# Opening slabs of four projections in pairs of chunks with 512 moving columns, and two low parts moved to GpSimd

## The chip, the core and the metric

The kernel runs on one core of a Trainium2 chip. The metric is device time in microseconds (us): 1195.06 us is the median of three runs (1194.7 to 1195.49).

## The reference

Everything is float32 on 256 tokens of 1024 features. The first block has two layers and a final norm, the second block one layer and a final norm; the second takes the first's output.

```python
# first block
x = x + even_mixer(rms_norm(x, norm_mix[0]), ...)    # neighbourhood attention (8 heads) and latent attention (8 heads)
x = x + sq_relu_mlp(rms_norm(x, norm_mlp[0]), ...)   # square(relu(xn @ w1)) @ w2, w1: 1024 x 4096
x = x + odd_mixer(rms_norm(x, norm_mix[1]), ...)     # dilated attention, 3 groups x 16 heads; w_in: 1024 x 9216
x = x + sq_relu_mlp(rms_norm(x, norm_mlp[1]), ...)
x = rms_norm(x, norm_final)
# second block
proj = rms_norm(x, mix_norm_gain_2) @ w_in_2         # to xa, ga (each 512), q, k, v (each 512), qx (512), gates (3072)
# linear recurrence on xa, causal attention on q k v, attention of qx to a memory of 256 tokens,
# three gated branches, w_out_2; then a gated feed-forward with a causal convolution, and a norm
```

The memory's keys and values, `rms_norm(mem_2) @ w_mem_kv_2`, depend on nothing else and are computed beside the first layer's attention.

## The kernel before

**Products in two parts.** For its precision the kernel splits each operand of a large product into a high part (rounded to the type that TensorE reads) and a low part (the rest), and adds three products: high by high, low by high, and high by low. A weight matrix is cut into 192 slabs of 1 MB, mostly 8 chunks of 128 rows by 256 columns, held in a ring of five raw buffers. SyncE loads slab n once slab n - 5 is released. ScalarE makes the high part (`high`, L1230; three buffers, so slab n needs slab n - 3 released). VectorE, or GpSimd for those slabs that `pooled` names, subtracts to get the low part (`low`, L1720 and L2486, on GpSimd in four pieces). `ahead(n)` means the split of slab n + 2; where it stands in an engine's program sets the order. Slabs 10, 12, 15, 17 (EVO) are the first layer's output projection, slabs 11, 13, 14, 16 (MEM) the memory's projection.

**The activations.** The high and the low part of the eight chunks of x lie side by side in XHL, 512 columns a chunk. ScalarE writes a high part (L1262), VectorE the low one from it (L1758, in the dilated order L1763).

**Three forms of a product with 256 columns of weights.**
- `features_by_chunks` (L695) takes two slabs together as the chunks of x come. Each slab has one bank of PSUM, its two halves of 128 features side by side. For each pair of chunks it issues high by high, low by high, high by low: for two slabs 96 matmuls of 256 moving columns, two banks.
- `beside` (L610, L615) gives each half slab a bank. The high weights are multiplied with XHL, 512 columns, so the bank's left half has high by high and its right half high by low; then the low weights add 256 columns to the left half. ScalarE copies the right half out (`copies`, L1286) and VectorE adds the left half to the copy (`added`, L1861). A bank is taken when VectorE has added it.
- `features_low_last` (L637) is the old form for slabs 2 to 5 of the third block, one bank a slab.

**Banks.** All eight PSUM banks go round in the order of use:

```python
i = turn_no[0] % 8
turn_no[0] += 1
if used[i] is not None:
    once.wait_ge(*at(("taken", *used[i])))
```

Uses other than slabs are `rows_back` (L909: transposes of the MLP's result, one bank each, added to x by VectorE at L1875), `last_rows_back` (two of these, issued between the first and second pair of chunks of the next product), the sums for a norm (L716, L720; one bank each), attention's scores, transposes and values.

**Order of work.** Each engine has its own program, run strictly in the order written; semaphores tie them. TensorE's order is: attention of the first layer with slabs between its steps, the MLP (`mlp`), the dilated part (`odd_slab`, i counts its 36 slabs), the second MLP, the third block's 12 slabs (IN2 = 122), its attention with the gates, the output projection, the feed-forward. `features_by_chunks` opens both MLPs, the dilated part and the third block. In the MLPs the pair is followed by ScalarE's Relu (L1364) and VectorE's square (L1893) for slabs 0 and 1, and by `copies`, `added` and one fused square (L1896) for the others. In the dilated part ScalarE copies a slab (L1526) for the exchange of rotary halves, and VectorE scales the slab out of PSUM (L2132; L2137 where `added` came first). In the third block VectorE runs `factors()` (L1747, L1753, L2224 to L2233: a mean, two reciprocals, four small operations, and one weight split within) and then `scaled` (L2215), which reads the slab and multiplies it with the factor. The feed-forward keeps `features_by_chunks`.

**Some waits of SyncE.** The exchange of rotary halves is four 64 KB transfers after ("copied", slab), queued before the slab load of its turn; the copy is of ScalarE before, and GpSimd multiplies what arrives (L2562).

The functions that the diff touches:

Of the kernel before, what the change touches and what calls it, by code (L numbers as in the profile page):

```python
# [336 lines left out]
def build(nc, A, out):  # L337
    with ExitStack() as ctx:
# [124 lines left out]
        def pooled(n):  # L463

            name = plan[n][0]
            if name == "od_o":
                return n >= ODO + 2
            if name == "branch":
                return sum(p[0] == "branch" for p in plan[:n]) > 1
            return name in ("out2", "fg")  # L470
# [101 lines left out]
        def tensor(pe):  # L572
# [128 lines left out]

            def tokens(n, x, late=False):
# [228 lines left out]
            def mlp(layer, norm, slot):  # L931
                features_by_chunks([W1[layer], W1[layer] + 1], x_ready(f"mlp{layer}"))
                row_sums(norm, slot)
                for j in range(2, 16):
                    beside(W1[layer] + j, x_ready(f"mlp{layer}"))
                down(layer, W2[layer])
# [123 lines left out]
            def odd_slab(i):  # L1060
                n, (kind, hb, g, k) = SLAB_ODD + i, DILATED[i]
                if i == 0:
                    features_by_chunks([n, n + 1], x, lambda: last_rows_back(0))
# [52 lines left out]
            for n in range(12):  # L1116
                if n == 0:
                    features_by_chunks([IN2, IN2 + 1], x, lambda: last_rows_back(1))
# [98 lines left out]
        def scalar(act):  # L1217
# [139 lines left out]
            def mlp(layer, norm, slot, follow):  # L1357
                for j in range(16):
# [3 lines left out]
                    if j < 2:  # L1362
                        b = take(("slab", W1[layer] + j))
                        act.activation(TA[j % 2][:, :], b[:, :], ACT.Relu).then_inc(  # L1364
                            *tell(s_act_out, ("taken", "slab", W1[layer] + j), ("relu", layer, j)))
                    else:
                        copies(W1[layer] + j, TB[j % 2], ("hlo", layer, j - 2))
                        ahead(W1[layer] + j + 1)
# [141 lines left out]
            def odd_slab(i, begun=False):  # L1510
# [13 lines left out]
                if i < 2:  # L1524
                    b = take(("slab", n))
                    act.activation(TA[k][:, :], b[:, :], ACT.Copy, scale=1.0).then_inc(*tell(s_act_out, ("copied", n)))  # L1526
                else:
                    copies(n, TA[k], ("rotated", swaps[0] - 2))
# [45 lines left out]
            for n in range(12):  # L1574
                if n != 1:
                    ahead(IN2 + n)
                if n == 0:
# [3 lines left out]
                    act.activation(RS[:, 0, 0:S + 2], RS[:, 0, 0:S + 2], ACT.Sqrt).then_inc(*tell(s_root, "both sqrt"))  # L1581
                if n == 7:
# [129 lines left out]
        def vector(dve):  # L1712
# [164 lines left out]
            def mlp(layer, norm, slot, follow, beside):  # L1877
                r = RS[:, slot, S:S + 2]
                for j in range(16):
# [11 lines left out]
                    if j < 2:  # L1891
                        once.wait_ge(*at(("relu", layer, j)))
                        dve.tensor_tensor(z, a, a, ALU.mult).then_inc(*tell(s_dve, ("h", layer, j)))  # L1893
                    else:
                        added(W1[layer] + j, a, z)
                        dve.scalar_tensor_tensor(out=z, in0=a, scalar=0.0, in1=a, op0=ALU.max, op1=ALU.mult).then_inc(  # L1896
                            *tell(s_dve, ("h", layer, j)))
# [210 lines left out]
            def odd_slab(i):  # L2108
# [5 lines left out]
                if 1 < i < EARLY:  # L2114
                    rotate(1)
                if i != 1:
                    ahead(n)
                rotate(1)
                if i == 0:
# [10 lines left out]
                if i < 2:  # L2130
                    b = take(("slab", n), [("copied", n)])
                    dve.tensor_tensor(to, pair(b[:, :]), twice(RP[:, 0:S]), ALU.mult).then_inc(  # L2132
                        *tell(s_dve_out, ("taken", "slab", n), ("scaled", n)))
                else:
                    v = TA[rotated[0] % 2]
                    added(n, v, v, ("copied", n))
                    dve.tensor_tensor(to, pair(v[:, :]), twice(RP[:, 0:S]), ALU.mult).then_inc(*tell(s_dve, ("scaled", n)))  # L2137
# [71 lines left out]
            def scaled(n, dst, by=1.0):  # L2209
                if n < IN2 + 8:  # L2210
# [264 lines left out]
        def gpsimd(pool):  # L2475
# [68 lines left out]
            for n in (EVO[2], MEM[3], EVO[3]):  # L2544
# [190 lines left out]
```

## Time and profile before

| | |
|---|---|
| median of 3 runs | 1195.06 us |
| the profiled execution | 1195.08 us |
| its span | 1193.3 us |
| TensorE, matmuls | 1184.5 us busy, 99% |
| TensorE, weight loads (beside the matmuls) | 1034.6 us, 87% |
| VectorE | 830.7 us, 70% |
| ScalarE | 658.5 us, 55% |
| GpSimd | 222.3 us, 19% |
| DMA queues | 54.6% of 16 engines, 214 MB |

A profile row gives the time of an instruction or of a run of like ones. The end of a matmul is modelled and includes its way through the array, so that successive matmuls overlap: their rate is read from start to start, or from the chain, which counts only the time to the next one. In all rows times are us from the span's start. In a timeline a row is: start, duration from first start to last end, engine, line, operation, output <- inputs, shapes, count, and in brackets an idle time of the engine before it and what ended it. Line numbers are those of the kernel before.

### The profile page before, as it was taken

The numbers are of one execution on the slowest core, as the hardware profiler recorded it, in microseconds if no ns is written. First come the engines' busy times: TensorE is split into PE (matmuls) and PEld (weight loads), VectorE is DVE, ScalarE is ACT, GpSimd is POOL, SyncE is SP. The second block draws the span as 40 slices with busy tenths as digits, with TensorE's granted clock in tenths as the row PEclk, the third lists the DMA queues.
The fourth block names the chain that finished last, engine by engine and source line by source line (L and its number), as shares of the span: only waits on it lengthen the run. The fifth ranks groups of instructions, "written<-read, shape, count | busy, mean of one in ns | idle before, by whom it ended". The sixth has DMA issues, their size and how long they took to land.

```text
span 1193.3 us, 18415 instructions
## 1 busy us (share of the span) xinstructions
PE 1184.5 (99%) x7409; PEld 1034.6 (87%) x7409; DVE 830.7 (70%) x1184; ACT 658.5 (55%) x899; POOL 222.3 (19%) x169
## 2 busy tenths in 40 slices
PE   9999999999999999999999999999999999999998
PEld 9989898888898888888988888897878899888886
DVE  7878777754576688765788844597966566676863
ACT  5584465533455655557565535456685555555452
POOL 2530010000011021200300000010010885544100
PEclk9999999999999999999999999999999999999999
DMA  9723456656558566664366565555544455565551
GB/s 265 244 83 130 141 177 186 203 178 205 182 165 273 187 211 193 202 204 140 110 190 198 178 204 184 185 183 176 178 144 166 149 194 177 182 195 188 176 195 53
DMA packets 158995, 214.04 MB, mean 179 GB/s; under 512 B 5259, under 2 KB 111054, under 8 KB 158910
## 3 DMA queue, kind: packets, MB, share of 16 engines
q1 hardware_dynamic: 158110, 211.41, 54.6%
q8 instruction: 59, 0.97, 0.3%
q10 hardware_dynamic: 608, 0.99, 0.3%
q0 software_dynamic: 192, 0.46, 0.2%
q14 instruction: 26, 0.21, 0.1%
HBM read 205.50 MB, written 1.05 MB: 173 GB/s over the span
## 4 chain that ended last, share of the span: by engine, by line
PE 93%; DVE 4%; ACT 2%; issue 1%; DMA 1%; SPq 0%; DVEq 0%; ACTq 0%
PE ps L595 44%; PE ps L610 22%; PE ps L615 11%; PE ps L695 4%; PE ps L792 2%; PE ps L843 2%; PE ps L637 2%; PE ps L800 1%; DVE wlo L1720 1%; PE ps L811 1%; PE ps L661 1%; ACT whi L1230 1%; DMA raw<-in_ev_w_in_dram 1%; DVE TA L2400 0%; PE ps L716 0%
## 5 line engine op out<-in xcount | busy, mean ns | idle before, releaser
L1720 DVE TENSOR_TENSOR wlo<-raw,whi 128x2048 fp32r<-128x2048 f32 (+1 forms) x167 | 384.5, 2304 | 148.9 <-ACT whi L1230 148.3
L1230 ACT ACTIVATE whi<-raw 128x2048 fp32r<-128x2048 f32 x188 | 357.9, 1907 | 154.4 <-PE ps L595 132.3
L610 PE MATMUL ps<-XHL,whi 128*128 128x512 f32 x1248 | 311.1, 393 | 0.0
L610 PEld LDWEIGHTS ps<-XHL,whi 128*128 128x128 f32 x1248 | 225.3, 189 | 42.1 <-DVE BIG L2132 0.5
L615 PEld LDWEIGHTS ps<-XHL,wlo 128*128 128x128 f32 x1248 | 167.8, 190 | 11.8 <-DVE wlo L1720 1.1
L615 PE MATMUL ps<-XHL,wlo 128*128 128x256 f32 x1248 | 171.5, 282 | 0.3 <-DVE wlo L1720 0.2
L2486 POOL TENSOR_TENSOR wlo<-raw,whi 128x512 fp32r<-128x512 f32 x88 | 119.1, 1388 | 157.3 <-ACT whi L1230 157.1
L595 PE MATMUL ps<-whi,HL 128*128 128x512 f32 (+1 forms) x416 | 144.8, 373 | 0.0
L595 PE MATMUL ps<-whi,HH 128*128 128x512 f32 x384 | 143.3, 390 | 0.0
L595 PE MATMUL ps<-whi,XHL 128*128 128x512 f32 (+1 forms) x480 | 139.7, 378 | 0.0
L595 PE MATMUL ps<-wlo,HH 128*128 128x512 f32 x368 | 139.4, 389 | 0.0
L595 PEld LDWEIGHTS ps<-whi,XHL 128*128 128x128 f32 x480 | 85.9, 188 | 15.9 <-issue 0.7
L2562 POOL TENSOR_TENSOR TB<-TB,BIG 128x512 f32<-128x512 f32 x24 | 38.6, 1607 | 324.3 <-DVE BIG L2126 189.1
L595 PEld LDWEIGHTS ps<-whi,HL 128*128 128x128 f32 x416 | 76.1, 188 | 13.6
L595 PE MATMUL ps<-wlo,XHL 128*128 128x512 f32 (+1 forms) x240 | 87.8, 375 | 0.0
L595 PEld LDWEIGHTS ps<-whi,HH 128*128 128x128 f32 x384 | 71.9, 188 | 14.7
L595 PEld LDWEIGHTS ps<-wlo,HH 128*128 128x128 f32 x368 | 69.0, 188 | 14.6 <-DVE wlo L1720 0.4
L1286 ACT ACTIVATE TB<-ps 128x256 f32<-128x256 f32 x82 | 29.3, 378 | 58.0 <-PE ps L615 56.2
L1286 ACT ACTIVATE TA<-ps 128x256 f32<-128x256 f32 x66 | 23.4, 380 | 57.5 <-PE ps L615 45.1
L595 PEld LDWEIGHTS ps<-wlo,XHL 128*128 128x128 f32 x240 | 44.2, 188 | 8.3
L1861 DVE TENSOR_TENSOR TA<-ps,TB 128x256 f32<-128x256 f32 x56 | 23.2, 421 | 25.0 <-ACT TB L1286 24.7
L1296 ACT ACTIVATE SN<-SN,stat 128x384 f32<-128x384 f32 (+2 forms) x64 | 34.4, 544 | 10.1 <-DVE stat L1789 10.1
(281 smaller groups left out, 1652.6 us busy)
## 6 DMA issues: line engine op xcount, KB each, us to landing
raw<-in_mlp_w_dram SPq DMA_DIRECT2D x64, 1024.0 KB, 5.3
raw<-in_od_w_in_dram SPq DMA_DIRECT2D x36, 1024.0 KB, 5.4
raw<-in_w_in_dram SPq DMA_DIRECT2D x24, 1024.0 KB, 5.1
raw<-in_w_ffn_gate_dram SPq DMA_DIRECT2D x12, 1024.0 KB, 5.1
raw<-in_w_ffn_up_dram SPq DMA_DIRECT2D x12, 1024.0 KB, 5.1
raw<-in_w_ffn_down_dram SPq DMA_DIRECT2D x12, 1024.0 KB, 5.0
TB<-TA SPq DMA_DIRECT2D x96, 64.0 KB, 2.4
raw<-in_w_branch_dram SPq DMA_DIRECT2D x6, 1024.0 KB, 4.9
```

The costliest lines, as they stand in the source:

```text
L595: m = pe.matmul(to, l[c][a], r[c][b], start=first and k == 0, stop=last and k == 3 * n - 1)
L610: pe.matmul(b[m][:, :], w[m][c][0], XHL[:, c, :], start=c == 0, stop=False)
L615: i = pe.matmul(b[m][:, 0:S], w[m][c][1], x[c][0], start=False, stop=c == 7)
L637: i = pe.matmul(b[:, m * S:m * S + S], w[m][c][a], x[c][z], start=m == c == a == z == 0, stop=m == a == 1 and c == len(x) - 1)
L695: i = pe.matmul(b[n][:, m * S:m * S + S], h[a], x[c][z], start=m == c == a == z == 0, stop=m == 1 and c == 7 and z == 1)
L792: m = pe.matmul(banks[u][rows, lo:hi], l, r, start=start, stop=stop)
L1230: act.activation(whi_of(n), raw_of(n), ACT.Copy, scale=1.0).then_inc(*tell(s_whi, ("whi", n)))
L1286: act.activation(to[:, m * S:m * S + S], b[:, S:2 * S], ACT.Copy, scale=1.0).then_inc(*tell(s_act_out, ("copy", n, m)))
L1296: m = act.activation(to[:, lo:hi], src[:, lo:hi], ACT.Exp, bias=st[:, k:k + 1], scale=-1.0 if biased else 1.0, accum_out=st[:, 2 + k:3 + k])
L1720: dve.tensor_tensor(wlo_of(n), raw_of(n), f32(whi_of(n)), ALU.subtract).then_inc(*tell(s_wlo, ("wlo", n)))
L2486: m = pool.tensor_tensor(lo[:, v], r[:, v], f32(hi[:, v]), ALU.subtract)
L2562: pool.tensor_tensor(z, z, twice(RP[:, S:512]), ALU.mult).then_inc(*tell(s_pool, ("sine", k)))
```

## The change

Four calls of `features_by_chunks` become calls of a new function, `pair_beside`, with four banks for two slabs. Its first pair of chunks goes (chunk 0 high weights), (0 low), (1 low), (1 high), the others low, low, high, high:

```diff
+            def pair_beside(ns, x, between=None):
+                b = {(n, m): bank(("beside", n, m)) for n in ns for m in range(2)}
+                w = {(n, m): w_ready(n, 8, m * P, P) for n in ns for m in range(2)}
+                for p in range(4):
+                    if p == 1 and between is not None:
+                        between()
+                    for c, a in ((0, 0), (0, 1), (1, 1), (1, 0)) if p == 0 else ((2 * p, 1), (2 * p + 1, 1), (2 * p, 0), (2 * p + 1, 0)):
+                        for n, m in b:
+                            for event in (w[n, m][c][2 + a], x[c][2], *((x[c][3],) if a == 0 else ())):
+                                once.wait_ge(*at(event))
+                            if a:
+                                pe.matmul(b[n, m][:, 0:S], w[n, m][c][1], x[c][0], start=False, stop=False)
+                            else:
+                                i = pe.matmul(b[n, m][:, :], w[n, m][c][0], XHL[:, c, :], start=c == 0, stop=c == 7)
...
-                features_by_chunks([W1[layer], W1[layer] + 1], x_ready(f"mlp{layer}"))
+                pair_beside([W1[layer], W1[layer] + 1], x_ready(f"mlp{layer}"))
...
-                    features_by_chunks([n, n + 1], x, lambda: last_rows_back(0))
+                    pair_beside([n, n + 1], x, lambda: last_rows_back(0))
...
-                    features_by_chunks([IN2, IN2 + 1], x, lambda: last_rows_back(1))
+                    pair_beside([IN2, IN2 + 1], x, lambda: last_rows_back(1))
```

What follows these products takes the form of the other slabs. MLP, ScalarE and then VectorE:

```diff
-                    if j < 2:
-                        b = take(("slab", W1[layer] + j))
-                        act.activation(TA[j % 2][:, :], b[:, :], ACT.Relu)...
-                    else:
-                        copies(W1[layer] + j, TB[j % 2], ("hlo", layer, j - 2))
+                    copies(W1[layer] + j, TB[j % 2], *([("hlo", layer, j - 2)] if j > 1 else []))
...
-                    if j < 2:
-                        once.wait_ge(*at(("relu", layer, j)))
-                        dve.tensor_tensor(z, a, a, ALU.mult).then_inc(*tell(s_dve, ("h", layer, j)))
-                    else:
+                    added(W1[layer] + j, a, z)
+                    dve.scalar_tensor_tensor(out=z, in0=a, scalar=0.0, in1=a, op0=ALU.max, op1=ALU.mult)...
```

Dilated part, VectorE (for the first two slabs the addition stands ahead of the next weight split; ScalarE makes two copies of the right halves in place of one of the whole):

```diff
+                if i < 2:
+                    v = TA[rotated[0] % 2]
+                    added(n, v, v, ("copied", n))
                 if i != 1:
                     ahead(n)
                 rotate(1)
```

Third block, ScalarE (behind the square root of the combined scale) and VectorE (in `scaled`, behind `factors()`):

```diff
+                if n < 2:
+                    copies(IN2 + n, PT[:, n, :])
...
             def scaled(n, dst, by=1.0):
-                if n < IN2 + 8:
+                if IN2 + 2 <= n < IN2 + 8:
                     b = take(("slab", n), ["both"])
                 else:
                     b = PT[:, (n - IN2) % 3, :]
                     added(n, b, b)
```

The low parts of slabs 14 (memory, third) and 15 (output projection, third) go from VectorE to GpSimd:

```diff
             name = plan[n][0]
+            if n in (EVO[1] + 2, MEM[1] + 2):
+                return True
...
-            for n in (EVO[2], MEM[3], EVO[3]):
+            for n in (EVO[1], MEM[1]):
                 ahead(n)
```

## Rows read from the trace of the kernel before

**Rows 1.** The page: TensorE's busy time, and the chain that ended last, by engine

```profile
PE   1184.5 (99%) x7409; PEld 1034.6 (87%) x7409; DVE 830.7 (70%) x1184; ACT 658.5 (55%) x899; POOL 222.3 (19%) x169
PE 93%; DVE 4%; ACT 2%; issue 1%; DMA 1%; SPq 0%; DVEq 0%; ACTq 0%
```

**Rows 2.** TensorE's waits: for whom, us in total, times, longest

```profile
PE ps L843 <- DVE PT L1812: 1.1, 2, 0.8
```

**Rows 3.** Timeline of TensorE around the second of these waits

```profile
127.76 0.28 PE L595 MATMUL ps<-wlo,HL 128*128 128x256 f32 x1
128.88 1.08 PE L843 MATMUL ps<-PT,BIG 128*64 128x256 f32 x8 [0.85 <-DVE PT L1812]
```

**Rows 4.** Timeline of VectorE: two weight splits, slab 14's first

```profile
111.84 2.29 DVE L1720 TENSOR_TENSOR wlo<-raw,whi 128x2048 fp32r<-128x2048 f32 x1
...
158.46 2.43 DVE L1720 TENSOR_TENSOR wlo<-raw,whi 128x2048 fp32r<-128x2048 f32 x1 [1.84 <-ACT whi L1230]
```

**Rows 5.** Timeline of ScalarE: the high part of slab 15

```profile
118.84 1.94 ACT L1230 ACTIVATE whi<-raw 128x2048 fp32r<-128x2048 f32 x1
```

**Rows 6.** Groups by line and shape: busy us, mean ns, idle before

```profile
L2486 POOL TENSOR_TENSOR wlo<-raw,whi 128x512 fp32r<-128x512 f32 x88 | 119.1, 1388 | 157.3 <-ACT whi L1230 157.1
L1861 DVE TENSOR_TENSOR TA<-ps,TB 128x256 f32<-128x256 f32 x56 | 23.2, 421 | 25.0 <-ACT TB L1286 24.7
```

**Rows 7.** The chain in order of time: start, us, what

```profile
39.49 3.65 PE ps L610 x16
43.14 1.91 PE ps L615 x16
...
149.44 11.72 PE ps L695 x96
...
589.19 11.59 PE ps L695 x96
```

**Rows 8.** Timeline of VectorE: low parts of x, both MLPs

```profile
149.37 0.88 DVE L1758 SCALAR_TENSOR_TENSOR XHL<-XT,V,XHL 128x256 fp32r<-128x256 f32 x2 [0.65 <-ACT XHL L1262]
...
589.35 2.70 DVE L1758 SCALAR_TENSOR_TENSOR XHL<-XT,V,XHL 128x256 fp32r<-128x256 f32 x4
```

**Rows 9.** Timeline of TensorE: the first product of both MLPs

```profile
149.41 1.19 PE L695 MATMUL ps<-XHL,whi 128*128 128x256 f32 x8
...
589.02 1.12 PE L695 MATMUL ps<-XHL,whi 128*128 128x256 f32 x8
```

**Rows 10.** Timeline of TensorE: high products of the fourth and the following slab, dilated

```profile
346.45 4.16 PE L610 MATMUL ps<-XHL,whi 128*128 128x512 f32 x16
...
352.36 3.82 PE L610 MATMUL ps<-XHL,whi 128*128 128x512 f32 x16
```

**Rows 11.** Timeline of VectorE: the scaling of the first two dilated slabs

```profile
347.75 1.29 DVE L2132 TENSOR_TENSOR BIG<-ps,BIG 128x512 f32<-128x512 f32 x2
```

**Rows 12.** Timeline of TensorE: slabs 2 and 4 of the third block begin

```profile
781.28 4.07 PE L637 MATMUL ps<-XHL,whi 128*128 128x256 f32 x32
...
792.87 4.00 PE L637 MATMUL ps<-XHL,whi 128*128 128x256 f32 x32
```

**Rows 13.** Timeline of VectorE: first and last step of factors(), and the first scaling

```profile
781.75 0.42 DVE L1747 TENSOR_SCALAR RS<-ps 128x258 f32<-128x258 f32 x1
...
789.59 0.43 DVE L2233 TENSOR_TENSOR RS<-RS 128x258 f32<-128x258 f32 x1
790.06 1.29 DVE L2215 SCALAR_TENSOR_TENSOR BIG<-ps,RS 128x512 f32<-128x512 f32 x2
```

**Rows 14.** Busy time by stretch at the kernel's end; PEclk is the granted clock

```profile
1187.00:1188.00 1.00, 0.41 (x2) 0.00 (x0) 1.00 (x2) 0.69 (x1) 0.00 (x0) 1.00 0.00 0
...
1191.00:1192.00 1.00, 0.00 (x0) 0.00 (x0) 0.00 (x0) 0.00 (x0) 0.00 (x0) 0.50 1.01 379
```

**Rows 15.** Timeline of TensorE: the same product at the start and later

```profile
1.04 4.64 PE L943 MATMUL ps<-ones 128*128 128x128 f32 x20 [1.04 <-DVE ones L1923]
...
7.07 1.60 PE L943 MATMUL ps<-ones 128*128 128x128 f32 x12
```

More of the change, by code:

```diff
@@ L700, in features_by_chunks @@
                     released[n] = [("product", "slab", n)]
+            def pair_beside(ns, x, between=None):
[12 more added lines that the diff above has]
+                                i = pe.matmul(b[n, m][:, :], w[n, m][c][0], XHL[:, c, :], start=c == 0, stop=c == 7)
+                            if c == 7 and a == 0:
+                                i.then_inc(*tell(s_product, ("product", "beside", n, m)))
+                for n in ns:
+                    released[n] = [("product", "beside", n, 1)]
             def tokens(n, x, late=False):
@@ L1361, in mlp @@
                         ahead(W1[layer] + 1)
-                    if j < 2:
-                        b = take(("slab", W1[layer] + j))
-                        act.activation(TA[j % 2][:, :], b[:, :], ACT.Relu).then_inc(
-                            *tell(s_act_out, ("taken", "slab", W1[layer] + j), ("relu", layer, j)))
-                    else:
-                        copies(W1[layer] + j, TB[j % 2], ("hlo", layer, j - 2))
+                    copies(W1[layer] + j, TB[j % 2], *([("hlo", layer, j - 2)] if j > 1 else []))
+                    if j > 1:
                         ahead(W1[layer] + j + 1)
@@ L1523, in odd_slab @@
                 k = swaps[0] % 2
-                if i < 2:
-                    b = take(("slab", n))
-                    act.activation(TA[k][:, :], b[:, :], ACT.Copy, scale=1.0).then_inc(*tell(s_act_out, ("copied", n)))
-                else:
-                    copies(n, TA[k], ("rotated", swaps[0] - 2))
+                copies(n, TA[k], *([("rotated", swaps[0] - 2)] if i > 1 else []))
                 swaps[0] += 1
@@ L1890, in mlp @@
                     a, z = TA[j % 2][:, :], TB[j % 2][:, :]
-                    if j < 2:
-                        once.wait_ge(*at(("relu", layer, j)))
-                        dve.tensor_tensor(z, a, a, ALU.mult).then_inc(*tell(s_dve, ("h", layer, j)))
[L1894 to L1897, printed above, removed]
+                    added(W1[layer] + j, a, z)
+                    dve.scalar_tensor_tensor(out=z, in0=a, scalar=0.0, in1=a, op0=ALU.max, op1=ALU.mult).then_inc(
+                        *tell(s_dve, ("h", layer, j)))
                     if j == 0:
@@ L2118, in odd_slab @@
                 rotate(1)
+                if i > 1:
+                    v = TA[rotated[0] % 2]
+                    added(n, v, v, ("copied", n))
                 if i == 0:
@@ L2129, in odd_slab @@
                 to = pair(QKV[hb % 3][3 * g + w])
[L2130 to L2137, printed above, removed]
+                v = TA[rotated[0] % 2]
+                dve.tensor_tensor(to, pair(v[:, :]), twice(RP[:, 0:S]), ALU.mult).then_inc(*tell(s_dve, ("scaled", n)))
                 if i >= EARLY:
```

## The prediction

> **What bounds the kernel now.** I read the page's busy shares first, then the chain that ended last, then the waits of TensorE, and last the timelines of the five places that the change touches. TensorE is busy for 99% of the span, and 93% of the chain runs through it [rows 1]. So the kernel is a queue of matmuls with hardly a hole: TensorE's longest entry in the waits is 1.1 us in two pieces, both for the copy of attention probabilities on VectorE [rows 2]. An edit can therefore gain only by shortening the stream of matmuls or by closing one of the few holes, and it loses one for one whatever it makes TensorE wait. VectorE (70%) and ScalarE (55%) have slack on the mean, which matters only where TensorE needs something of theirs.
>
> The sum is made against the profiled execution: 1195.08 us, of which 1193.3 are its span. The median of the three timed runs is 1195.06, so nothing has to be shifted between the two. Differences under 0.2% (2.4 us) can't be told from no change.
>
> **Part 1, two low parts on GpSimd.** Slabs 14 and 15 are split on GpSimd, in four pieces of 1.39 us each [rows 6], instead of one VectorE subtraction of 2.3 us each. VectorE did slab 14's at 111.84 [rows 4] and slab 15's in the same way between the two holes, each in front of the reductions, outputs and probability copies for which TensorE then waited. Taking away 2.2 us ahead of the first wait and 4.4 ahead of the second is more than both waits hold. The recorded waits are 1.1 us; from the issue times the second hole alone is 128.88 - 127.76 - 0.12 = 1.0 [rows 2, 3]. I take 1.25 us of gain, bounds 0.8 and 1.5. Is the low part late? The high part of slab 15 is ready at 118.84 + 1.94 = 120.8, GpSimd ends at 120.8 + 4 x 1.39 = 126.4, and slab 15 is multiplied only after the values and transposes issued from 128.88 [rows 3, 5, 6]. Slab 14 has more room. GpSimd has nothing else to do between the rotary keys and the squares of the first MLP. So no wait replaces the ones removed.
>
> The Trainium skill ("GPSIMD Engine Reference", Key points) speaks against such a move: GpSimd shares its SBUF interfaces with VectorE and contends with instructions that have two SBUF inputs. The trace shows a little of it: the VectorE subtraction that began at 158.46, with GpSimd at work, took 2.43 us instead of 2.29 [rows 4]. By that ratio (6%) some 8 us of VectorE work beside GpSimd would lengthen by 0.5 us, which the 4.4 us it was relieved of cover; the sum stays.
>
> **Part 2, the pair products.** Before, two slabs took 96 matmuls of 256 columns; after, 32 of 512 and 32 of 256, the same columns in fewer instructions. In the chain 16 matmuls of 512 take 3.65 us and 16 of 256 take 1.91, so a pair costs 2 x 3.65 + 2 x 1.91 = 11.12 us; the 96 took 11.72 and 11.59 in the two MLPs [rows 7]. The gain is 0.47 to 0.60 us a pair, and there are four pairs.
>
> The Trainium skill ("TensorE: Matmul & The Clock Gate", Back-to-back issue gap) gives N/2.4 + 2.5 ns for the isolated spacing. By it 32 instructions fewer are 0.08 us. Here 1.91/16 - 256/2.4 is 12.7 ns, so the measurement decides.
>
> Where does the gain go? The new order opens with a product of the high weights with both parts of chunk 0, so it needs chunk 0's low part; the old one needed the high part alone.
> - First MLP: the low parts of chunks 0 and 1 are two operations of 0.88 us together from 149.37, so chunk 0's ends at about 149.85, and the first matmul goes at about 149.98 instead of 149.41. That is 0.57 later, against 0.47 to 0.6 shorter [rows 7 to 9]. With the later chunks (the pair needs two more of them every 11.12 / 4 = 2.8 us, and the old run of 11.72 us with the same steps had hardly a hole) nothing more is late. I take +0.1.
> - Second MLP: there the four low parts begin at 589.35, after a weight split, and the old code began at 589.02. First matmul at about 589.96: +0.94 - 0.47 = +0.5 [rows 7 to 9].
> - In both MLPs VectorE gets two additions of 0.42 us [rows 6] for each of the two slabs and keeps its square. That is 1.6 us more ahead of the split of slab 5 of the MLP. By my walk along the queue it keeps 1 us of room in the first MLP and nearly none in the second, where the decay steps are interleaved. I count 0, bounds 0 and 0.4.
> - Dilated part: chunk 0's two parts are long there. The shorter pair ends 0.47 earlier, but the fourth slab's second half already waited for a bank: 16 matmuls took 4.16 us instead of 3.82, released by the first rotary scaling, which began at 347.75 [rows 10, 11]. Before, that bank was freed when the scaling had read it. Now the pair takes four banks, and the same matmul needs the third of them, free when the scaling (1.29 us for two, so about 0.69 for the first) and then the first addition of the next slab (0.42) are done: 347.75 + 1.11 = 348.86 against about 348.4. The gain is eaten and 0.4 us lost: +0.4, bounds -0.4 and +0.8.
>
> **Part 3, the third block, which decides.** TensorE gives its eight PSUM banks out in rotation and waits until the last user of the next one was read. I write down the order from the end of the second MLP. Before: two banks of the down product, two of rows back, slabs 0 and 1, two of rows back, sums n4 and n5 (these take the down banks), slabs 2 and 3 (the first rows-back banks), slab 4 (slab 0's bank). After: two down, two rows back, four of the pair (0a, 0b, 1a, 1b), two rows back (down banks), n4 and n5 (the first rows-back banks), and slab 2 takes bank 0a. So slab 2 can't start until half 0a is read, by the first half of the new addition. In VectorE's order this addition stands after factors(), which computes the combined scale. Before, slab 2 began at 781.28 with factors() under way, and only slab 4, nearly 12 us later, wanted a bank that factors() holds. Factors() runs from 781.75 to 789.59 + 0.43, and the scaling that freed slab 0 began at 790.06 [rows 12, 13].
>
> Now the first addition of 0.42 us stands there: 790.0 + 0.42 + 0.1 = 790.5. Nothing in the queue of factors() gets earlier by more than 0.1 us, for it hangs on the squares and on the last split, not on the pair. ScalarE's copy of the right halves goes behind the square root and is long done by 790. So TensorE resumes at 790.5 instead of 781.28: +9.2 us, the pair's own gain of 0.5 being inside that wait. Bounds 8.7 and 9.7. Slabs 3, 4 and 5 take banks 0b, 1a and 1b, freed 0.4 to 2 us later, in time. That VectorE is ahead afterwards is of no use: TensorE has no other wait to give back [rows 2].
>
> **Part 4, the clock.** TensorE would stand still from about 780.8 to 790.5. At the kernel's end it ran out of work at 1187.4 and the granted clock was 0.50 (its 1.2 GHz level) from 1191 to 1192 [rows 14]. The stall is a longer rest than that one, so it should restart at the lower level. What does a restart cost? The start shows it: 20 matmuls of one form in 4.4 us from 1.04 (to 5.47), while later 12 of the same form took about 1.6, or 2.7 us for 20 [rows 15]. The loss is 1.8 us for records of 128 columns; with 4.4 us at half rate and an overhead that doesn't double, 2.0. I take 2.0, bounds 0 and 3.5 (a restart that stays low half as long again, and more).
>
> **Sum.** -1.25 + 0.1 + 0.5 + 0.4 + 9.2 + 2.0 = +10.95. 1195.08 + 10.95 = 1206.0 us.
>
> **The rivals.**
> - Stall, but no cold restart (1204.0). For it: no row shows a fall in mid-kernel. Against it: the end of the kernel [rows 14]. Chance 0.15. The reverse, a longer time at the low level, would give up to 1207.5 and is part of the forecast's range.
> - No stall (faster). The mechanism: slab 2 of the third block doesn't land on a bank of the pair, because my count of uses between is off by two, or a bank of the pair is read before factors(). It decides at the point where slab 2 needs its bank, 780.9. Then the four pairs give back what they can (third block -0.5, dilated -0.45 with the same miscount, MLPs +0.6) and part 1 gives 1.25: 1193.5 us. For it: TensorE never waited there before. Against it: the same count explains the dilated wait [rows 10, 11], and puts slab 4 on slab 0's bank at 792.87, after its release, with no wait seen [rows 12, 13]. Chance 0.05.
> - No stall, but the dilated wait and a late split in the second MLP: 1195, within 0.2%. Chance 0.03.
> The forecast itself has 0.77. Faster by over 0.2%: 0.05. Same: 0.03. Slower: 0.92. The range reaches from the stall with a short cold restart to a stall with a long one and late splits: 1203.2 to 1208.4.
>
> **What would show it.** One wait of TensorE of 9 to 10 us at the first L637-type matmul of the third block, released by the VectorE addition that follows the last multiplication of factors(), with the granted clock at 0.5 for some of the following 5 us. The pair products as 64 matmuls in about 11.1 us. The waits for the probability copy at 120 and 128.9 gone. The first MLP's pair starting about 0.6 us and the second's about 0.9 us later after the last row product. In the dilated part a longer wait at the second half of the fourth slab. The forecast is wrong if TensorE goes from the n5 sums into the third slab without waiting.

## The result, and the profile after

The changed kernel takes 1211.7 us (median of 4 runs, 1211.07 to 1211.98), the kernel before 1195.28 us in the same measurement (1194.7 to 1196.16). The ratio is 1.0136, 95% interval 1.0124 to 1.0148: 16.4 us slower. The profiled execution took 1211.65 us, 1209.9 of it in its span, which was 1193.3 before. All times below that stand against each other are of profiled executions, unless a median is named.

The page of the changed kernel, busy times and the chain by engine, answers to [rows 1]:

```profile
PE 1187.9 (98%) x7281; PEld 1031.1 (85%) x7281; DVE 837.8 (69%) x1198; ACT 660.2 (55%) x909; POOL 229.8 (19%) x177
PE 94%; DVE 3%; ACT 1%; issue 1%; DMA 0%; SPq 0%; DVEq 0%; ACTq 0%
```

128 matmuls are gone, yet TensorE is busy 3.4 us longer: some of the remaining ones ran slower. The other 13.2 us of the longer span are idle time of TensorE. Its waits (for whom, us in total, times, longest), which answer to [rows 2]:

```profile
PE ps L639 <- DVE PT L1877: 9.4, 1, 9.4
PE ps L718 <- DVE XHL L1774: 2.4, 2, 1.8
PE ps L822 <- DVE XT L1884: 1.5, 1, 1.5
PE ps L965 <- DVE ones L1935: 1.0, 1, 1.0
PE ps L612 <- DVE TA L1877: 0.8, 1, 0.8
PE ps L663 <- ACT whi L1411: 0.7, 2, 0.4
PE ps L822 <- DVE SN L1820: 0.3, 1, 0.3
```

L965 is the start of the kernel, as before. The one long wait is the forecast one, in the third block. The two of L822, the third row and the last, were not forecast; they stand in the place of the two waits that part 1 removed.

Where the time went is read from the chain, by the start of the same long piece in both kernels at the end of each stage:

| stage, up to | before | after | longer by | forecast |
|---|---|---|---|---|
| memory's first slab, behind its row sums (start-up) | 96.58 | 96.99 | 0.41 | 0 |
| first MLP's down product | 239.83 | 243.12 | 2.9 | -1.25 (part 1) + 0.1 (pair) |
| dilated part's last slabs | 514.95 | 518.64 | 0.4 | 0.4 |
| second MLP's down product | 679.44 | 684.80 | 1.7 | 0.5 |
| third block's output product | 966.95 | 983.80 | 11.5 | 9.2 + 2.0 |
| feed-forward's down product | 1121.84 | 1138.41 | -0.3 | 0 |

The start-up moves by some tenths between executions of all kernels here (95.8 to 97.3), so its 0.4 us is not put down to the change.

**The third block.** VectorE and then TensorE in the changed kernel, answering to [rows 12, 13]:

```profile
787.03 0.42 DVE L1763 TENSOR_SCALAR RS<-ps 128x258 f32<-128x258 f32 x1
...
794.86 0.43 DVE L2245 TENSOR_TENSOR RS<-RS 128x258 f32<-128x258 f32 x1
795.33 0.76 DVE L1877 TENSOR_TENSOR PT<-ps,PT 128x256 f32<-128x256 f32 x2
```

```profile
785.95 0.50 PE L742 MATMUL ps<-ones,SQ 128*128 128x1 f32 x4
795.81 6.39 PE L639 MATMUL ps<-XHL,whi 128*128 128x256 f32 x32 [9.35 <-DVE PT L1877]
```

TensorE ends the row sums at 786.45 and stands until the first half of the addition (795.33 + 0.42) has read bank 0a. ScalarE's copies were done at 792.5, so the addition waited for factors() and not for them. The following 32 matmuls take 6.39 us, where 32 of the same form took 4.07 before [rows 12].

**The clock.** Busy time by stretch, TensorE first; the third column from the end is the granted clock. Of the changed kernel, around slab 13 and around the stall:

```profile
114.00:116.00 2.00, 1.71 (x9) 1.47 (x10) 1.90 (x4) 0.00 (x0) 0.00 (x0) 0.73 0.00 0
116.00:118.00 2.00, 2.00 (x11) 2.00 (x11) 1.76 (x5) 0.83 (x4) 0.00 (x0) 0.50 0.00 0
118.00:120.00 2.00, 2.00 (x17) 2.00 (x17) 0.11 (x1) 2.00 (x9) 0.00 (x0) 0.91 0.00 0
...
792.00:794.00 2.00, 0.00 (x0) 0.00 (x0) 2.00 (x2) 2.00 (x3) 0.00 (x0) 0.50 0.17 62
796.00:798.00 2.00, 2.00 (x10) 2.00 (x11) 1.93 (x5) 0.00 (x0) 0.00 (x0) 0.50 0.03 8
800.00:802.00 2.00, 2.00 (x15) 2.00 (x14) 1.89 (x5) 0.00 (x0) 0.00 (x0) 0.75 0.00 0
802.00:804.00 2.00, 2.00 (x19) 2.00 (x18) 0.28 (x1) 0.00 (x0) 0.00 (x0) 1.00 0.00 0
```

At 0.50 (the 1.2 GHz level) ten matmuls go in two microseconds, at 1.00 nineteen. The low level is seen twice: after the stall, as forecast, and at slab 13, at 115, where nothing had been forecast. Both stand in the chain as longer pieces (start, us, what). The second answers to 23.13 us for the same 192 matmuls before. The first answers to 6.01 to 6.02 us in those of the later kernels that have the same waits and in which the clock stayed at 1.00:

```profile
114.95 7.50 PE ps L597 x48
...
795.81 25.59 PE ps L639 x192
```

**The first MLP's approach.** VectorE, and GpSimd, at slab 13's inputs in the changed kernel; L2498 is slab 14's low part, part 1 of the change:

```profile
109.54 2.50 DVE L1820 TENSOR_SCALAR SN<-SN,stat 128x256 f32<-128x256 f32 x2
112.15 1.42 DVE L1820 TENSOR_SCALAR SN<-SN,stat 128x256 f32<-128x256 f32 x2
113.50 2.84 DVE L1884 TENSOR_TENSOR XT<-XT,ps 128x512 f32<-128x512 f32 x4
```

```profile
107.79 5.38 POOL L2498 TENSOR_TENSOR wlo<-raw,whi 128x512 fp32r<-128x512 f32 x4 [27.21 <-ACT whi L1252]
```

The four normalisations of attention weights take 3.9 us; four of the same shape away from GpSimd take about 0.35 each. Three began under GpSimd's pieces and are long; the last began when GpSimd had ended (107.79 + 5.38 = 113.17) and is short (0.34). TensorE waits 0.3 us for the second of them, which it transposes next. Its next four transposes then want a bank that the first addition onto x (XT) frees. This addition stands behind all four normalisations in VectorE's queue, and TensorE waits 1.5 us for it.

**Both MLPs' pairs.** TensorE's first product of each, answering to [rows 9]:

```profile
153.04 1.16 PE L718 MATMUL ps<-XHL,whi 128*128 128x512 f32 x4 [0.56 <-DVE XHL L1774]
...
594.67 1.16 PE L718 MATMUL ps<-XHL,whi 128*128 128x512 f32 x4 [1.80 <-DVE XHL L1774]
```

VectorE's low parts of x in both, answering to [rows 8], and GpSimd at the second:

```profile
152.41 0.88 DVE L1774 SCALAR_TENSOR_TENSOR XHL<-XT,V,XHL 128x256 fp32r<-128x256 f32 x2 [0.65 <-ACT XHL L1284]
...
593.04 2.67 DVE L1774 SCALAR_TENSOR_TENSOR XHL<-XT,V,XHL 128x256 fp32r<-128x256 f32 x4
```

```profile
592.87 1.37 POOL L2510 TENSOR_TENSOR SQ<-SQ 128x512 f32<-128x512 f32 x1 [14.01 <-ACT SQ L1268]
```

From their first matmul to the row sums behind them the pairs took 11.24 and 11.26 us (11.12 forecast). The first waited 0.56 us as forecast; the second 1.8, since the first low part of chunk 0 ended at 594.5, 1.5 us after it began.

**Dilated part.** TensorE at the second half of the fourth slab, and the VectorE addition that frees its bank, answering to [rows 10, 11]:

```profile
352.18 2.14 PE L612 MATMUL ps<-XHL,whi 128*128 128x512 f32 x8 [0.75 <-DVE TA L1877]
```

```profile
351.71 0.75 DVE L1877 TENSOR_TENSOR TA<-ps,TA 128x256 f32<-128x256 f32 x2
```

### The profile page after: what moved, and what is told of

Same layout as the page of the kernel before. It is cut to its first block, busy times and chain, and to the rows that moved or that the text cites. A ratio compares the mean times of both kernels' runs of the same rounds, so it can differ in the third digit from the quotient of the medians.

```text
span 1209.9 us, 18209 instructions
## 1 busy us (share of the span) xinstructions
PE 1187.9 (98%) x7281; PEld 1031.1 (85%) x7281; DVE 837.8 (69%) x1198; ACT 660.2 (55%) x909; POOL 229.8 (19%) x177
## 4 chain that ended last, share of the span: by engine, by line
PE 94%; DVE 3%; ACT 1%; issue 1%; DMA 0%; SPq 0%; DVEq 0%; ACTq 0%
PE ps L597 43%; PE ps L612 23%; PE ps L617 12%; PE ps L814 2%; PE ps L865 2%; PE ps L639 2%; PE ps L718 2%; PE ps L822 1%; PE ps L716 1%; DVE wlo L1736 1%; PE ps L833 1%; PE ps L663 1%; DMA raw<-in_ev_w_in_dram 0%; PE ps L697 0%; ACT whi L1252 0%
## 5 line engine op out<-in xcount | busy, mean ns | idle before, releaser
L1736 DVE TENSOR_TENSOR wlo<-raw,whi 128x2048 fp32r<-128x2048 f32 (+1 forms) x165 | 379.3, 2300 | 155.4 <-ACT whi L1252 154.7
L617 PEld LDWEIGHTS ps<-XHL,wlo 128*128 128x128 f32 x1248 | 167.7, 190 | 11.7 <-DVE wlo L1736 1.0
L2498 POOL TENSOR_TENSOR wlo<-raw,whi 128x512 fp32r<-128x512 f32 x96 | 129.7, 1383 | 192.8 <-ACT whi L1252 192.6
L2574 POOL TENSOR_TENSOR TB<-TB,BIG 128x512 f32<-128x512 f32 x24 | 35.4, 1474 | 328.2 <-DVE BIG L2144 189.4
L1877 DVE TENSOR_TENSOR TA<-ps,TB 128x256 f32<-128x256 f32 x64 | 25.9, 421 | 22.6 <-ACT TB L1308 22.3
```

What stands on the lines that cost most here:

```text
L617: i = pe.matmul(b[m][:, 0:S], w[m][c][1], x[c][0], start=False, stop=c == 7)
L1736: dve.tensor_tensor(wlo_of(n), raw_of(n), f32(whi_of(n)), ALU.subtract).then_inc(*tell(s_wlo, ("wlo", n)))
L1877: dve.tensor_tensor(to[:, v], b[:, 0:S], copy[:, v], ALU.add).then_inc(*tell(s_dve_out, ("taken", "beside", n, m), *(events if m else ())))
L2498: m = pool.tensor_tensor(lo[:, v], r[:, v], f32(hi[:, v]), ALU.subtract)
L2574: pool.tensor_tensor(z, z, twice(RP[:, S:512]), ALU.mult).then_inc(*tell(s_pool, ("sine", k)))
```

## The experiments

Two theories of part 1 stood first. H: while a GpSimd instruction runs, VectorE's normalisations are held, and part 1 loses. P: part 1 gains as predicted, and the loss at 112 to 122 comes from something else of the change. On the stall there were three. B: TensorE waits for the bank that the addition frees. F: with that bank free early, the wait only moves to a later bank. R: the third block holds more of the excess than the stall and its restart. The clock's price came next.

**lows_only**: the kernel before with part 1 alone.

```diff
+            if n in (EVO[1] + 2, MEM[1] + 2):
+                return True
 ...
-            for n in (EVO[2], MEM[3], EVO[3]):
+            for n in (EVO[1], MEM[1]):
                 ahead(n)
```

> The kernel before with part 1 alone: slabs 14 and 15 get their low parts on GpSimd. Theory H (GpSimd holds VectorE: while a GpSimd subtraction runs, VectorE's operations on SBUF between 109 and 114 us stand until it ends, the transposes come late, TensorE rests and its clock falls): TensorE is 2.4 us late at slab 13, the 48 matmuls of that slab take about 7.5 us instead of 5.75, the two later holes vanish; 1195.1 + 2.5 = 1197.6 us. Rival P (what the prediction said: the low parts are off the path, and the loss seen in this stage of the changed kernel comes from its other edits): two holes vanish, 1193.8 us.

Measured: 1197.98 us (median of 10 runs, before 1195.21), ratio 1.002, interval 1.0011 to 1.0029. TensorE's waits in this kernel, two of its five rows:

```profile
PE ps L802 <- DVE XT L1870: 1.5, 1, 1.5
...
PE ps L802 <- DVE SN L1806: 0.3, 1, 0.3
```

H holds, P falls: the moved subtractions alone bring the same two waits and cost 2.8 us of median. Here slab 13's 48 matmuls took 6.02 us, not the 7.5 expected: the clock did not fall. In the profiled execution the stage up to the first MLP's down product is therefore only 1.1 us longer (144.39 for 143.25). Of the other 1.6 us of its span, 0.9 lie in the feed-forward (155.83 for 154.89) and 0.7 in the start-up. That the median comes near the 1197.6 expected is luck, for the slow clock of that sum did not come and the feed-forward's part was not in it.

**lows_late**: the same, but GpSimd starts each low part only when the normalisations of its slab's stretch are done.

```diff
-            for n in (EVO[1], MEM[1]):
+            for n, u in ((EVO[1], 11), (MEM[1], 13)):
+                once.wait_ge(*at(("soft", u)))
                 ahead(n)
```

> Part 1 alone, but GpSimd starts each of the two low parts only after VectorE has normalised the softmax units of that step (10 and 11, then 12 and 13). GpSimd's work is the same, only its place moves by about 2 us. Theory H: what VectorE does beside it now are sums onto x and reductions that read PSUM, which are not held; TensorE doesn't wait at slab 13, its clock stays, the two old holes vanish: 1193.8 us, some 3.5 us less than with GpSimd early. Rival W (any GpSimd work beside VectorE costs it about as much, or the low parts themselves come late): 1196 to 1198 us as before the move.

Measured: 1195.1 us (10 runs), ratio 0.9999 (0.999 to 1.0008), 2.9 us less than lows_only by the medians, but 1.3 more than H had expected. VectorE and GpSimd in this kernel:

```profile
109.38 0.62 DVE L1806 TENSOR_SCALAR SN<-SN,stat 128x256 f32<-128x256 f32 x2
...
110.10 0.62 DVE L1806 TENSOR_SCALAR SN<-SN,stat 128x256 f32<-128x256 f32 x2
110.63 2.84 DVE L1870 TENSOR_TENSOR XT<-XT,ps 128x512 f32<-128x512 f32 x4
```

```profile
110.85 5.03 POOL L2488 TENSOR_TENSOR wlo<-raw,whi 128x512 fp32r<-128x512 f32 x4 [30.46 <-DVE SN L1806]
```

The normalisations are back at 0.35 us each, and both waits are gone. The same GpSimd pieces now run beside the XT additions, which read PSUM, and these still take 2.84 us for four: not every VectorE operation is held. From the row sums (96.83) to the first MLP's down product (238.81) the kernel takes 1.3 us less than the one before, which is the gain that part 1 was predicted to have (1.25). The feed-forward gives it back (156.07 us for 154.89). There the chain runs through VectorE and ScalarE from 1012 on, in the kernel before only from 1065 on, and TensorE waits 0.8 us for a low part instead of 0.2. It is not that this stage keeps its end when something comes earlier: it is as long in lows_only (155.83) and lows_small (155.87), which do not reach it earlier in the same way (2 us later and 0.1 us earlier), and both have the same wait of 0.8 us. All kernels built on the changed one have 154.6 to 154.9. So part 1 on the kernel before goes with some 1 us in the feed-forward, and no run shows why.

**lows_small**: lows_only with eight pieces of 256 columns in place of four of 512, to see whether the hold goes by the length of the GpSimd instruction.

```diff
-                for q in range(4):
-                    v = slice(512 * q, 512 * q + 512)
+                w = 256 if n in (EVO[1] + 2, MEM[1] + 2) else 512
+                for q in range(2048 // w):
+                    v = slice(w * q, w * q + w)
```

> Part 1 alone with GpSimd early, but in eight pieces of 256 columns for these two slabs instead of four of 512. Theory H in its exact form (a VectorE operation that meets a GpSimd subtraction stands until that one instruction ends): each of the four normalisations of 109 to 113 us is held for at most 0.7 us instead of up to 1.35, so TensorE's wait for the transposes shrinks from 1.5 to under 0.5 us, the clock stays, and the time is 1195.5 to 1196.5 us. Rival S (the two share a path and both are slowed all the while GpSimd works): the hold is as long as with four pieces, and the time 1198 us.

Measured: 1196.33 us (10 runs, before 1195.12), ratio 1.0011 (1.0002 to 1.002). The four normalisations of 108.8 to 111.1 in this kernel (min/median/max in ns), and TensorE's wait for what follows them:

```profile
L1806 DVE TENSOR_SCALAR SN<-SN,stat x4: 628/812/819, 108.8 to 111.1; 128x256 f32<-128x256 f32 x4
```

```profile
PE ps L802 <- DVE XT L1870: 0.9, 1, 0.9
```

GpSimd in this kernel:

```profile
107.09 6.06 POOL L2489 TENSOR_TENSOR wlo<-raw,whi 128x256 fp32r<-128x256 f32 x8 [27.22 <-ACT whi L1232]
```

Its pieces take 6.06/8 = 0.76 us instead of 5.38/4 = 1.35, and the longest normalisation is 0.82 us instead of 1.36. So VectorE is held until the GpSimd instruction under way ends, once for each of its own instructions. The wait of 0.9 us is more than the 0.5 I had allowed: the sum over four normalisations falls only from 3.9 to 2.9, since all four are held now (0.63 to 0.82). The stage is 1.0 us shorter than in lows_only (143.38 for 144.39). Had the two engines merely slowed each other for as long as GpSimd works (rival S), smaller pieces would have changed nothing.

**block3_old**: the changed kernel with the third block as before.

```diff
-                    pair_beside([IN2, IN2 + 1], x, lambda: last_rows_back(1))
+                    features_by_chunks([IN2, IN2 + 1], x, lambda: last_rows_back(1))
...
-                if n < 2:
-                    copies(IN2 + n, PT[:, n, :])
...
-                if IN2 + 2 <= n < IN2 + 8:
+                if n < IN2 + 8:
```

> The changed kernel with the third block's opening as before (96 matmuls of 256 columns, two banks, the old scaling). Theory B (slab 2 waits for a bank of the pair until factors() is done, and the clock falls in that rest): both go, 9.0 us of wait and 2.5 us of slow clock: 1211.6 - 11.5 = 1200.1 us. Rival R (the rest of the excess over the prediction sits in this block too, so that undoing it gives back more): 1197 us or less.

Measured: 1199.96 us (5 runs), ratio 1.0039 (1.0025 to 1.0053). The change less this is 11.7 us, and the stage is at 287.50 us again (before 287.51, after 299.00). B holds and R falls: part 3 alone is 70% of the loss, and the whole of what the third block lost.

**in2_front**: the changed kernel, pair and all, with both additions put ahead of factors() and both copies ahead of the first root.

```diff
                 if n == 0:
+                    copies(IN2, PT[:, 0, :])
+                    copies(IN2 + 1, PT[:, 1, :])
                     root("n4", 1, cols=True)
...
-                    added(n, b, b)
+                    if n >= IN2 + 8:
+                        added(n, b, b)
...
+                    for k in range(2):
+                        added(IN2 + k, PT[:, k, :], PT[:, k, :])
                     ahead(IN2)
                     factors()
```

> The changed kernel with the third block's four bank-freeing additions moved ahead of the weight split and factors() on VectorE, and the copies ahead of the square root on ScalarE. Four banks stay. Theory B: they are free at about 786, when TensorE asks, so neither the wait of 9.35 us nor the slow clock is left: 1211.7 - 11.8 = 1199.9 us, as with the old third block, though factors() ends 1.5 us later. Rival F (factors() being later only moves the wait to the next user of its scale, the fifth or sixth slab's bank): a new wait of 1 us or more and 1201 us or more.

Measured: 1199.42 us (5 runs, before 1195.12), ratio 1.0035 (1.0022 to 1.0048). TensorE and VectorE in this kernel:

```profile
785.95 4.08 PE L639 MATMUL ps<-XHL,whi 128*128 128x256 f32 x32
```

```profile
784.73 1.55 DVE L1877 TENSOR_TENSOR PT<-ps,PT 128x256 f32<-128x256 f32 x4 [0.99 <-ACT PT L1308]
```

Slab 2 follows the sums without a wait and at full rate. B holds, F falls: nothing but the place of the additions in VectorE's queue (and of the copies ahead of them) made the stall. The pair itself is worth nothing there: the stage takes 287.53 us, as with the old products. Slab 2 starts 0.3 us earlier in the stage than before, and this is gone at the first product behind the 192 matmuls. TensorE's weight loads (PEld) stand there for the low part of a weight, which VectorE makes; the kernel before had no wait at this place:

```profile
809.74 0.19 PEld L597 LDWEIGHTS ps<-wlo,XHL 128*128 128x128 f32 x1 [0.47 <-DVE wlo L1736]
```

**filler**: the changed kernel with 32 products of a matrix of ones in the stall (64 matmuls of 7.39 us in the trace), written to a bank that is free and not read, so that TensorE doesn't rest for most of it.

```diff
                     sums("n5", 0, cols=True)
+                    once.wait_ge(*at(("taken", "back", 1, 2)))
+                    for _ in range(32):
+                        pe.matmul(ps[bank_of.get(("back", 1, 2), 0)][:, 0:P], ones[:, :], ones[:, :], start=True, stop=True)
```

> The changed kernel with 32 products of ones behind the sums of the third block, written to a bank that is free (their results are not read): some 8.5 us of work in the 9.35 us in which TensorE stands still. The output is the same. If the slow clock after the stall is a price of its own, that TensorE's rest sets, the granted clock stays at 1.00 there and the time falls by 2.4 us to 1209.2. If the wait alone is the loss and the slower matmuls of slab 2 have another reason (transfers or copies beside them), it stays at 1211.6.

Measured: 1208.74 us (4 runs, before 1195.21), ratio 1.0112 (1.0096 to 1.0127). This kernel after the stall, TensorE's timeline and a stretch:

```profile
794.50 4.09 PE L639 MATMUL ps<-XHL,whi 128*128 128x256 f32 x32 [2.09 <-DVE PT L1880]
```

```profile
796.00:798.00 2.00, 2.00 (x19) 2.00 (x18) 1.97 (x3) 0.00 (x0) 0.00 (x0) 1.00 0.00 0
```

TensorE resumes at the same point of the stage (111.0 us into it in both), but at full clock, and the stage is 2.3 us shorter (296.68). That is the price of the restart, taken by itself: with the clock kept, the same matmuls beside the same work run at full rate. The stage is the measure here and in sq_wait, not the median: the four times of filler lie 2.8 us apart and those of sq_wait 3.6, where the changed kernel's lie within 0.9, and the fall of the clock at slab 13, worth 1.5 us, is missing in both profiles.

**sq_wait**: the changed kernel, with GpSimd's square additions before the second MLP held back until the low parts of x are done.

```diff
+            once.wait_ge(*at(("xlo", "mlp1", 3)))
             for j in range(1, 4):
                 add_square("n3", 0, j, j == 3)
```

> The changed kernel, but before the second MLP GpSimd adds its first squares only when VectorE has written the low parts of chunks 0 to 3. Theory H: in the changed kernel the first of these low parts took 1.49 us instead of 0.48 because GpSimd's addition began 0.17 us before it; now it takes 0.48, TensorE's wait at the second MLP falls from 1.8 to 0.8 us, and the time by 1.0 to 1210.7. Rival M (that operation is long for another reason, as the first one after a weight split): it stays at 1.5 us and so does the time.

Measured: 1209.91 us (4 runs, before 1195.12), ratio 1.0125 (1.0111 to 1.0138). TensorE, VectorE and GpSimd in this kernel:

```profile
591.70 1.16 PE L718 MATMUL ps<-XHL,whi 128*128 128x512 f32 x4 [0.79 <-DVE XHL L1774]
```

```profile
591.08 1.67 DVE L1774 SCALAR_TENSOR_TENSOR XHL<-XT,V,XHL 128x256 fp32r<-128x256 f32 x4
```

```profile
592.82 1.30 POOL L2510 TENSOR_TENSOR SQ<-SQ 128x512 f32<-128x512 f32 x1 [15.93 <-DVE XHL L1774]
```

Four low parts take 1.67 us instead of 2.67, the wait is 0.8 us instead of 1.8, and the stage is 1.0 us shorter: the term I had mis-sized, undone. That the first low part is long for standing behind a weight split (the rival) is ruled out: it still stands there, and takes 0.48 us. The profiled execution is 2.6 us shorter than the changed kernel's (1209.05 for 1211.65): 1.0 of it is this stage, and 1.5 is slab 13, where the clock didn't fall this time (6.02 us for 7.50).

**best**: every remedy together: lows_late, in2_front and sq_wait on the changed kernel, the second dilated slab's addition right behind the first's, and a pair that opens with three products of 256 columns of chunk 0, so that its low part is asked for last.

```diff
-                if i < 2:
-                    v = TA[rotated[0] % 2]
-                    added(n, v, v, ("copied", n))
+                if i == 0:
+                    for k in range(2):
+                        added(n + k, TA[k], TA[k], ("copied", n + k))
...
+                    if p == 0:
+                        for a, z in ((0, 0), (1, 0), (0, 1)):
+                            for n, m in b:
+                                once.wait_ge(*at(w[n, m][0][2 + a]))
+                                once.wait_ge(*at(x[0][2 + z]))
+                                pe.matmul(b[n, m][:, z * S:z * S + S], w[n, m][0][a], x[0][z], start=a == z == 0, stop=False)
```

> All mended together: GpSimd's low parts after the normalisations (-1.3 against before), the third block's additions ahead of factors(), the second dilated slab's addition right behind the first's (its bank free before the fourth slab wants it), GpSimd's squares held back at the second MLP, and each pair opening with the three 256-column products of chunk 0, so that chunk 0's low part is needed 0.95 us later. With nothing late, each of four pairs is 0.4 us shorter than 96 matmuls: 1195.2 - 1.3 - 4 x 0.4 = 1192.3 us. If the feed-forward (where VectorE's and ScalarE's chain is as long as TensorE's) gives 1 us back, as it did with the late low parts alone: 1193.5.

Measured: 1194.07 us (11 runs, 1192.28 to 1196.51; before 1195.12), ratio 0.9993, interval 0.9984 to 1.0002: not to be told from the kernel before, and above both expectations. The profiled execution is the shortest of the eleven, 1192.28 us. TensorE's waits, all of them but one of 1.0 us at the start:

```profile
PE ps L663 <- ACT whi L1417: 0.6, 2, 0.3
PE ps L617 <- DVE wlo L1742: 0.3, 1, 0.3
```

With the long waits gone, two of the four stages with a pair still take what they took before: 164.50 us for the second MLP (before 164.49), 287.56 for the third block (287.51). The dilated stretch is 0.6 us shorter, and from the row sums to the first MLP's end it is 1.5, of which lows_late alone had 1.3. Where the 0.5 us of a pair goes in the other two is seen at the weight loads. In the second MLP they wait 0.53 us for the low part of a weight, in the third block 0.47, and neither wait is in the kernel before:

```profile
616.66 1.01 PEld L617 LDWEIGHTS ps<-XHL,wlo 128*128 128x128 f32 x8 [0.53 <-DVE wlo L1742]
...
801.88 0.19 PEld L597 LDWEIGHTS ps<-wlo,XHL 128*128 128x128 f32 x1 [0.47 <-DVE wlo L1742]
```

TensorE comes earlier there, but VectorE's split does not. The prediction had seen this danger for the second MLP: it left the split "nearly none" of its room, with a bound of 0.4 us.

## Why the direction was right and the size was not

The forecast was 1206.0 us, range 1203.2 to 1208.4; it came to 1211.7, 5.7 us more. Taken term by term:

- **The stall of 9.2 us: right, in its mechanism and size.** The order of banks was read off rightly. TensorE reached slab 2 by 9.17 us later in its stage than before, released by the addition behind factors(); block3_old and in2_front take it away from two sides.
- **The restart of 2.0 us: right, a little small.** The 192 matmuls behind it took 25.59 us for 23.13, so 2.46; filler shows 2.3. The granted clock was 0.50 for some 5 us.
- **First MLP +0.1, dilated part +0.4: right.** Measured 0.26 (filler's stage of 144.65 against lows_only's 144.39, the clock kept in both) and 0.4, with the waits where they were said to be.
- **Part 1, -1.25: wrong, and the step that failed.** "So no wait replaces the ones removed." One did. In the table's terms part 1 is +2.6: slab 13 begins 2.4 us later and takes 1.5 longer, the clock having fallen; the two old holes closed, as I had said, and give 1.3 back. lows_only shows that part 1 brings the waits by itself, lows_late that only its place beside the normalisations does, lows_small that the hold goes by the length of GpSimd's instruction. This term is 3.9 of the 5.6 us that the sum missed in the profiled executions (16.6 for 10.95). 2.4 of the 3.9 are the waits (+1.1 in lows_only, where -1.25 was forecast). The other 1.5 are the clock at slab 13, which did not fall in every execution with the same waits; that it fell in the profiled one was not to be foreseen from any row.
- **How it failed.** I priced the contention by one ratio: a VectorE subtraction at 158.46 that took 6% longer [rows 4]. It was no measure of work beside GpSimd. GpSimd's last instruction there ended at 158.74, so the two were together for 0.28 of the 2.43 us, and 0.14 of them were lost:

```profile
158.01 0.73 POOL L2501 TENSOR_TENSOR SQ<-SQ 128x256 f32<-128x256 f32 x1
```

  A long instruction that is held once by the end of a GpSimd piece shows a small ratio; a short one shows a factor of four. The count of short instructions beside GpSimd should have been multiplied by the length of GpSimd's, not the VectorE time by a ratio. The trace of before had this very pair of operations elsewhere, which I had not looked for: its normalisations at 928 (min/median/max in ns), one of them beside the GpSimd piece that began at 928.42.

```profile
L1804 DVE TENSOR_SCALAR SN<-SN,stat x2: 354/860/1366, 928.2 to 928.5; 128x256 f32<-128x256 f32 x2
```

- **Second MLP, +0.5: mis-sized, 1.7.** I took the four low parts at even length and had the first one end 0.5 us after its start. By [rows 8] four took 2.70 us where two of the other MLP's took 0.88, so four 1.76; the missing microsecond lay wholly in the first, behind a GpSimd square addition. The old order didn't need that part; the new one opens with it. sq_wait gives back 1.0 of the 1.2 us. It is the same mechanism as part 1's.
- **What the rule would have given.** I quoted only that the two engines contend. The Trainium skill ("SBUF — State Buffer", SBUF: two separate sides) says more: the shared pair of ports is an exclusive lock, had by whichever instruction starts first for its whole length, while the other blocks; VectorE wants it with two inputs in SBUF, against a GpSimd instruction that reads SBUF, or with one input in a two-port mode. "VectorE: DVE Perf Modes" (Mode 2×_2P) counts an fp32 tensor_scalar from SBUF to SBUF among the latter. The runs agree on all four kinds of operation seen here: the normalisations (one SBUF tensor, up to 1.36 us for 0.35) and the low parts of x (two, 1.49 for 0.48) were held, each by one GpSimd instruction at most; the XT additions, with one input in PSUM, were not; and the long subtraction of [rows 4] lost 0.14 us, which as a ratio says nothing. By that rule, and the pieces of 1.39 us of [rows 6], an estimate was to be had before any run: three or four normalisations held for 1.39 - 0.35 = 1.04 us each, 3 to 4 us on VectorE's queue.
- **The range** held a long restart and late splits, but took no bound for part 1 on the side of a loss (a gain of 0.8 us was its worst). Four normalisations each held for the rest of a GpSimd piece, 4 x 1.0 us in place of the gain of 1.25, would have put that end at 1206.0 + 1.25 + 4.0 = 1211.3 by itself. That it comes near the measured time is partly luck: TensorE was late by 2.4 us, not by 4, and the clock at slab 13 and the second MLP added what this bound leaves out.

## What to carry to other kernels

Before moving work to GpSimd, list the short VectorE instructions that will run beside it and have all their tensors in SBUF, as the two forms that were held here, and charge each the rest of one GpSimd instruction; look in the trace for the same two forms side by side, by the spread between the median and the longest of a line, not by a mean. When a product takes more accumulation banks, write out the rotation and find which reader frees the bank that the next product lands on; if that reader stands behind a long chain in its engine's queue, move it ahead of the chain. In a stream without holes a cheaper product at one place is worth only what the rest of its stage lets through: here pairs that are 0.5 us shorter gave nothing in two of their four stages, where the next low part of a weight was not ready sooner.

## What the runs showed of the hardware that was not expected

- A VectorE normalisation (tensor by a scalar per partition, 128x256, SBUF to SBUF) went from 0.35 to as much as 1.36 us beside GpSimd pieces of 1.35 us, and to 0.82 beside pieces of 0.76; the low part of x (scalar_tensor_tensor) from 0.48 to 1.49. Additions and reductions that read PSUM kept their length beside the same GpSimd work (2.84 us for four additions both in lows_late and with GpSimd idle).
- After a wait of 0.3 and one of 1.5 us, with four short transposes between them, the granted clock fell to 0.50 in three executions (the changed kernel, block3_old, in2_front; 7.50 to 7.52 us for 48 matmuls) and not in three others with the same waits (lows_only, filler, sq_wait; 6.01 to 6.02). What decides between them was not found. After the stall of 9.35 us it fell both times it was profiled, and the restart cost 2.3 to 2.5 us.
- 32 products of 128 columns in that stall (64 matmuls in the trace, 7.39 us) kept the clock at 1.00 through a remaining wait of 2.1 us.
